# Feed-forward stage with stationary h: when the last block's values are turned, and where both copying engines put the weight copies of the first and the last block

## The reference

```python
D_MODEL, SEQ, DEPTH, D_FF = 1024, 256, 2, 2816

def rms_norm(x, g):
    xf = x.astype(jnp.float32)
    y = xf * lax.rsqrt(jnp.mean(xf * xf, axis=-1, keepdims=True) + EPS)
    return (y * g.astype(jnp.float32)).astype(x.dtype)

def swiglu(h, w_gu, w_down):
    gate, up = jnp.split(h @ w_gu, 2, axis=-1)
    return (jax.nn.silu(gate) * up) @ w_down

for i in range(DEPTH):
    x = x + 0.5 * swiglu(rms_norm(x, norm_ffn1[i]), w_ffn1_gu[i], w_ffn1_down[i])
    ...
    x = x + mix
    x = x + 0.5 * swiglu(rms_norm(x, norm_ffn2[i]), w_ffn2_gu[i], w_ffn2_down[i])
    gate = jax.nn.sigmoid(rms_norm(x, norm_ple[i]) @ w_ple_gate[i])
    x = x + gate * (p[i] @ w_ple_proj[i])
```

## Time and profile before

| | us |
|---|---|
| median of 3 runs | 1755.27 |
| lowest and highest run | 1751.82, 1755.93 |
| the profiled execution's own time | 1752.62 |
| its span, first to last instruction | 1750.9 |
| PE busy in it | 1675.1 (96%) |
| DVE, ACT, POOL busy in it | 1026.1, 809.7, 160.4 |
| mean granted TensorE clock | 0.978 of full |

### The profile page before, as it was taken

One profiled execution on the slowest core, in us unless ns is written; L12 is line 12 of the kernel. 1 busy time (PEld: TensorE's weight loads), 2 busy tenths in 40 slices (PEclk: granted clock), 3 DMA queues, 4 the chain that ended last, 5 costly groups with the idle time before them and its releaser, 6 DMA issues.

```text
span 1750.9 us, 25261 instructions
## 1 busy us (share of the span) xinstructions
PE 1675.1 (96%) x10262; PEld 1479.6 (85%) x10262; DVE 1026.1 (59%) x995; ACT 809.7 (46%) x978; POOL 160.4 (9%) x121
## 2 busy tenths in 40 slices
PE   7999999899999999999999999888999999999998
PEld 6888886788889788888888998666899989888997
DVE  6454676364547554577445686665566567556563
ACT  5343457353435544355434544444544455444442
POOL 1000123110002100012000135111000000000000
PEclk9999999999999999999999999778999999999999
DMA  7545451155453554555454353202255534335551
GB/s 293 202 171 189 156 185 69 73 203 212 172 188 145 193 186 174 192 191 188 169 204 172 139 213 127 93 24 87 106 194 191 187 150 178 114 119 182 181 190 48
DMA packets 39625, 282.14 MB, mean 161 GB/s; under 512 B 4417, under 2 KB 4545, under 8 KB 5761
## 3 DMA queue, kind: packets, MB, share of 16 engines
q1 hardware_dynamic: 39168, 279.59, 43.3%
q0 software_dynamic: 384, 1.51, 0.2%
HBM read 280.04 MB, written 1.05 MB: 161 GB/s over the span
## 4 chain that ended last, share of the span: by engine, by line
PE 82%; DVE 8%; ACT 5%; DMA 2%; issue 2%; POOL 1%; SPq 0%; DVEq 0%; POOLq 0%; ACTq 0%
PE ps L319 25%; PE ps L322 25%; PE ps L323 25%; DVE w_lo L1385 2%; DMA raw<-weights 2%; ACT w_hi L1019 1%; PE ps L501 1%; DVE hT_lo L1397 1%; ACT arena L1198 1%; PE ps L715 1%; PE ps L671 1%; DVE arena L1676 0%; DMA arena<-nsa_tables 0%; ACT arena L1049 0%; DVE arena L1617 0%
## 5 line engine op out<-in xcount | busy, mean ns | idle before, releaser
L1385 DVE TENSOR_TENSOR w_lo<-raw,w_hi 128x2048 fp32r<-128x2048 f32 x264 | 600.5, 2298 | 168.6 <-ACT w_hi L1019 168.5
L1019 ACT ACTIVATE w_hi<-raw 128x2048 fp32r<-128x2048 f32 x264 | 495.9, 1906 | 59.3 <-DMA raw<-weights 53.8
L319 PE MATMUL ps<-w_hi,hT_hi 128*128 128x512 f32 (+1 forms) x984 | 383.2, 389 | 15.4 <-DVE hT_lo L1397 13.9
L323 PE MATMUL ps<-w_hi,hT_lo 128*128 128x512 f32 (+1 forms) x984 | 376.9, 383 | 0.0
L322 PE MATMUL ps<-w_lo,hT_hi 128*128 128x512 f32 (+1 forms) x984 | 376.3, 382 | 0.0
L319 PE MATMUL ps<-hT_hi,w_hi 128*128 128x256 f32 x984 | 281.5, 286 | 7.7 <-DVE hT_lo L1397 4.9
L322 PE MATMUL ps<-hT_lo,w_hi 128*128 128x256 f32 x984 | 278.4, 283 | 0.0
L323 PE MATMUL ps<-hT_hi,w_lo 128*128 128x256 f32 x984 | 278.4, 283 | 0.0
L319 PEld LDWEIGHTS ps<-w_hi,hT_hi 128*128 128x128 f32 x984 | 185.9, 189 | 50.7 <-DVE w_lo L1385 11.2
L323 PEld LDWEIGHTS ps<-w_hi,hT_lo 128*128 128x128 f32 x984 | 185.7, 189 | 36.6
L322 PEld LDWEIGHTS ps<-w_lo,hT_hi 128*128 128x128 f32 x984 | 185.9, 189 | 32.9 <-issue 0.2
(11 more groups left out here) (263 smaller groups left out, 1872.1 us busy)
## 6 DMA issues: line engine op xcount, KB each, us to landing
raw<-weights SPq DMA_DIRECT2D x264, 1024.0 KB, 4.8
X<-x SPq DMA_DIRECT2D x2, 512.0 KB, 6.9
out<-X SPq DMA_DIRECT2D x4, 256.0 KB, 2.1
arena<-p POOLq DMA_DIRECT2D x2, 256.0 KB, 5.3
arena<-counts POOLq DMA_DIRECT2D x1, 512.0 KB, 6.5
arena<-nsa_tables POOLq DMA_DIRECT2D x1, 448.0 KB, 7.0
const<-constants SPq DMA_DIRECT2D x1, 427.0 KB, 9.7
cols<-parameters SPq DMA_DIRECT2D x1, 213.5 KB, 2.5
```

Of the source, the lines that this page charges most:

```text
L319: mm = nc.tensor.matmul(dst, a_hi, b_hi, start=start, stop=False, skip_group_check=True)
L323: return nc.tensor.matmul(dst, a_lo, b_hi, start=False, stop=stop, skip_group_check=True)
L1019: nc.scalar.activation(unit_cols(w_hi, u, 0, UNIT), raw[:, r * UNIT:(r + 1) * UNIT], ACT.Copy).then_inc(hi_done.sem, 1)
L1385: nc.vector.tensor_tensor(unit_cols(w_lo, u, 0, UNIT), raw[:, r * UNIT:(r + 1) * UNIT], f(unit_cols(w_hi, u, 0, UNIT)), ALU.subtract).then ...
```

## The change

Three places move; no instruction is added or taken away.

- TensorE: the last block is turned in front of quarter 2 of down(9) instead of quarter 3.
- The last block on ACT and DVE: units u0+34 and u0+35 (the second and third unit of the following stage) were both copied behind `hid_hi` / `hid_lo` of the last block. Now the first is copied ahead of the block's two silus (ACT) and two products (DVE), the second between those and `hid_hi` / `hid_lo`.
- The first block on ACT: the stage's sixth unit was copied ahead of block 0's silus (`split_to(u0 + 6)` before the stage). Now it is copied behind them, ahead of `hid_hi`. DVE's order is the same there.

```diff
@@ TensorE, ffn
-                one(FFN_BLOCKS - 1, u, mid={1: lambda: turn(FFN_BLOCKS - 2)}, in_down={3: lambda: turn(FFN_BLOCKS - 1)})
+                one(FFN_BLOCKS - 1, u, mid={1: lambda: turn(FFN_BLOCKS - 2)}, in_down={2: lambda: turn(FFN_BLOCKS - 1)})
                 down(u + 3, HC, False, True)
@@ ScalarE, ffn, one(j, u, t)
                     b0 = 2 * (j % 2)
+                    last = j == FFN_BLOCKS - 1
+                    ahead = u + 2 + RING
+                    if last:
+                        split_to(ahead - 2)
                     act.wait_ge(*gu_full.due(me, turn=t))
...
-                    last = j == FFN_BLOCKS - 1
-                    ahead = u + 2 + RING
-                    if not last and j:
+                    if j:
                         split_to(ahead - 1, t)
+                    else:
+                        split_to(u0 + 6)
                     act.wait_ge(*rows_turned.due(me, turn=t))
                     nc.scalar.activation(chunk(hid_hi, HC if last else 0, HC), bank(b0), ACT.Copy).then_inc(hid_hi_done.sem, 1)
-                    split_to(ahead - 1 if last else ahead, t)
+                    if not last:
+                        split_to(ahead, t)
@@ ScalarE, ahead of each stage
-                split_to(u0 + {"mlp": 6, "ffn": 6}.get(kind, 5))
+                split_to(u0 + {"mlp": 6}.get(kind, 5))
```

## The result

| | before | after |
|---|---|---|
| median of 4 runs each | 1755.22 us | 1736.56 us |
| lowest, highest run | 1751.82, 1755.93 | 1732.70, 1738.15 |
| ratio of the times, 95% interval | | 0.9894 [0.9873, 0.9915] |
| profiled execution: own time, span | 1752.62, 1750.9 | 1737.39, 1735.7 |
| PE busy | 1675.1 | 1669.3 |

The kernel became 1.06% faster, 18.7 us by the medians and 15.2 by the two profiles. The forecast was 13.4 us and 1741.9, with a range from 1736.5 to 1747.5, so the time lies at its very edge: right in kind, short in size.

A forecast was written before the change was run, and what follows sets the result against it. TensorE, busy 96% of the span, was taken as the bound, so only its standing time could be won: 5.0 + 0.9 + 7.5 = 13.4 us, from a median of 1755.3 to 1741.9 us, range 1736.5 to 1747.5.

The forecast's parts named there:

- Place A: Block 0 of the ffn stages: TensorE's waits ahead of turn(0) in the first three vanish, 5.0 us.
- the spot that I called tightest: Block 0 of the third ffn stage: DVE's products end just before TensorE wants the turn, 0.2 us to spare.
- Places B and C: Down(10)'s wait for `hid_lo` goes, 0.9 us; TensorE's standing at the start of the next stage goes, 7.5 us.
- The squares: POOL's additions of squares become TensorE's next wait: gain 8.8 us, time 1746.5; chance 0.15, shared with losing part of Place A.
- The waits at block 0 stay: Products at block 0 late for another reason: Place A gives 2.3 us or nothing, 1744.6 to 1746.9; part of a shared 0.15.
- the adds to X are not what TensorE waits for: Start of the next stage: something else holds it, so place C gives nothing, gain 5.9 us, 1749.4; chance 0.05.
- Slower: Moved copies push the last block: up to 2.3 us slower, 1757.6; chance 0.04 gain eaten, 0.03 slower by over 0.3%.
- place C: Start of the stage behind each ffn stage: TensorE's standing behind down(10), 1.57 or 2.16 us each, goes, 7.5 us.

The follow-up runs named there:

- a_again: The changed kernel once more, nothing altered, compared with the kernel before: 1732.75 us, ratio 0.9886.
- e_f3_old: The changed kernel with the sixth unit's copy back ahead of block 0's silus in the third ffn stage alone: 1742.76 us, ratio 0.9931 to before.
- e_both: The changed kernel with both unit copies of the last block together between silus and `hid_hi`, products and `hid_lo`: 1743.11 us, ratio 0.9939 to before.
- e_turn1: The changed kernel with the last block's turn one quarter earlier still, ahead of quarter 1 of down(9): 1737.63 us, ratio 0.9892 to before.
- e_turn: The kernel before with only the last block's turn one quarter earlier: 1742.42 us against 1754.8, ratio 0.9937.
- e_turn_last: The changed kernel with the first block of every ffn stage as before: 1745.13 us, ratio 0.9942 to before.
- e_turn_2: The kernel before with only the last block's turn one quarter earlier, a second look of one execution: 1748.02 us.
- e_last: The kernel before with only the last block's unit copies moved ahead of `hid_hi` and `hid_lo` on both engines: 1745.0 us, ratio 0.9946.
- e_first: The kernel before with only ACT's sixth unit copy moved behind block 0's silus: 1747.41 us, ratio 0.9954.
- b_again: The kernel before, unaltered, once more for its profile, one execution: 1751.13 us.
- b_null: The kernel before compared with itself: 1754.75 us against 1754.62, ratio 1.0004.
- e_f3_old_2: The changed kernel with the sixth unit's copy at its old place in the third ffn stage alone, one more execution: 1736.1 us.

## Why the prediction was right, and where it was short

**Place A, forecast 5.0 us.** The gaps fell by 1.13 + 1.11 + 2.72 = 4.96. Right, with the spot that I called tightest holding by 0.4 us. Undone in one stage, it cost that stage's 2.7 us again.

**Places B and C, forecast 0.9 + 7.5 = 8.4 us.** From the table F1, F2 and F4 are 2.1, 2.5 and 2.5 us shorter, and F3 is 3.85, less the 1.6 of its low stretch 2.3: 9.3 in all. The cause was right in each stage, and the size is 0.9 us short. Some 0.3 of that can be seen: behind the wait ahead of down(10) the next step is longer too, 0.20 where 0.12 is usual, in each of the four stages, which I counted as the usual step. The other 0.6 can't be explained: in some stages a block of 96 matmuls and a turn takes 17.02 us, in others 16.99, 0.3 us over a stage; all four stages of the changed kernel have the short one, F1 and F3 of before the long one. Why is open.

**The term that was missing.** My sum had no term for the clock: the step of place A had priced F3's wait as 2.7 us and the clock was read only in the page's slices of 44 us, in which 3.5 us at half speed don't show. Behind the wait another 1.6 us were lost. With it the sum is 4.96 + 9.3 + 1.6 = 15.9, and the profiles' F4 ends are 16.0 apart. The rest of the program then gave back 0.8, which makes the 15.2 of the spans.

**And from 15 to 18.7.** The stick stage of the first profile of before took 159.5 us; the two later ones of the same kernel took 161.3 and 163.4. In after, `a_again` and the four others that were built from the changed kernel with its first block in F1 and F2 (`e_f3_old` twice, `e_both`, `e_turn1`) it took 159.3 to 159.7. The mean of F4's end is 988.1 us over the three executions of before and 969.9 over the two of after, 18.2 apart. That is close to the medians' 18.7 but doesn't explain them, because the rest of the program was shorter in two of the three, 755 us against 759.4: the whole spans of these five executions are 15.1 apart. The ten runs of the changed kernel have a median of 1734.9, and both profiled ones, 1737.39 and 1737.34, are longer; the three profiled ones of before are shorter than the medians of that kernel, 1754.6 to 1755.2. So 3 us or more of the medians' difference lie in executions that no profile shows, and stay open. Whether the change itself favours the short stick stage, by where the low stretches of the clock fall in it, or whether six in a row are luck, the runs don't settle: `e_turn` and `e_turn_last` had the short one too, `e_turn_2`, `e_last` and `e_first` the middle one. That the first median came to lie inside the stated range, by 0.06 us, is luck as well: the second, 1732.75, is 3.75 us under its low end. The sum without a term for the clock was too small for both.

**The rivals.** *The squares* did not come up: PE waited for them once, 0.2 us, as before. In the ple stage behind F2 the sum stands at 539.12, and the additions are through well ahead of it; from the timeline of POOL:

```profile
530.26 2.77 POOL L1982 TENSOR_TENSOR arena<-arena 128x512 f32<-128x512 f32 x2 [173.95 <-ACT arena L1039]
534.10 1.57 POOL L1982 TENSOR_TENSOR arena<-arena 128x512 f32<-128x512 f32 x1 [1.06 <-ACT arena L1039]
535.75 0.75 POOL L1983 TENSOR_TENSOR arena<-arena 128x256 f32<-128x256 f32 x1
```

The three took 1.4 to 1.6 us each, the half addition 0.75, and 2.6 us of cover are left. The work that stands beside them did get longer: `hT_lo` took 1.92 for a pair at 199.77 in F1, 0.87 for the pair at 198.32. By the rule of the Trainium skill ("SBUF — State Buffer", Who interferes with whom) that a VectorE instruction with two inputs in SBUF and a GpSimd instruction that reads SBUF exclude each other, one has to wait for the other. The pair fits that: POOL's additions began at 200.04, within the longer pair and behind the shorter one. The price was nothing here, as TensorE needs those chunks microseconds later. *The waits at block 0 stay* and *the adds to X are not what TensorE waits for* fell with the waits' rows. *Slower* did not happen, but `e_both` shows its mechanism at work: the same two copies, put together in one place, cost 1.7 to 1.9 us a stage.

**The parts are not a sum.** Alone, by the medians, they gave 12.4, 9.8 and 7.4 us, 29.6 together, against 18.7 and 21.9 for all at once. By the profiles the turn and the copies share 1.1 to 1.3 us at each place C, and each median holds its own share of clock stretches as well.

## What to carry to other kernels

When an engine that others depend on copies ahead of need, look at what stands behind each copy in its order, at the seams between stages first: here some 14 us came from three copies and four transposes that moved by a few places, with no instruction less. Fill the engine's idle stretch of each block with one copy, not two in one gap, and count the cover on the chain that is wanted next. And when you price a wait of TensorE of over two microseconds, look at the clock in one-microsecond stretches behind it: what the wait costs may not end with the wait. Read it in more than one execution: here the same wait of the same program was followed by the low clock in one and not in the other.

## What was not expected of the hardware

- A wait of 2.4 to 2.6 us ahead of F3's turn (2.8 to 2.95 between starts) was followed, in five of nine profiles, by some 3.5 us at 1.2 GHz, beginning 0.4 to 1.4 us behind the turn's start. It cost 1.6 us each time: from turn(0) to turn(1) it took 14.55 to 14.61 us with it, 12.97 to 13.00 in the other four, whose clock stayed at 1.00 behind the same wait, in `e_f3_old_2` for a program that had fallen in its other execution.
- Of the eight gaps of 2.2 to 2.3 us ahead of a ple stage (`before`, `b_again`, `b_null`, `e_first`) two were followed by it, in `e_first` behind F2 (1.5 us lost) and in `b_null` behind F4. So place C, too, can cost more than its wait; in the profile that the forecast rests on it did not. Gaps of 0.5 to 1.9 us in F1 and F2 never brought a stage that was longer by over 0.4 us.
- In the stages with many short waits the low stretches lie differently from one execution to the next: the stick stage took 159.3 to 163.4 us, and all behind F4 either 753.6 to 755.3 or 758.7 to 760.1, in no relation to the edits. In the 140 us that begin 100 us behind F4's end the mean granted clock is 0.80 in before and 0.82 in after, both of the longer kind, and 0.87 in `e_both`, of the shorter. Of a difference of a few microseconds between two executions this makes a good part; the ffn stages of one program, where no such stretch falls in them, repeat to 0.4 us.
